# Input projections of a hybrid decoder layer: 576 tokens split as 256 and 320 columns in place of 288 and 288

## The reference, cut to what matters

```python
proj = jnp.einsum('btd,de->bte', x, w_in)            # d = 1024, e = 4096
q, k, v, g_att, gb, gc, hh, g_conv = jnp.split(proj, ...)   # 512 features each
o_att = _dilated_attention(q, k_all, v_all, offset).reshape(bsz, t, D_ATT)
att = o_att * jax.nn.silu(g_att)
u = gc * hh
y_conv = conv_w[0] * u_pad[:, 0:t] + ...              # width 3, causal, depthwise
z = gb * y_conv * jax.nn.silu(g_conv)
out = jnp.einsum('bte,ed->btd', jnp.concatenate([att, z], axis=-1), w_out)
y = _layer_norm(DEEPNORM_ALPHA * x + out, ln_g, ln_b)
```

## Time and profile before

| what | value |
|---|---|
| time, median of 3 runs (lowest to highest) | 361.42 us (359.41 to 361.47) |
| span of the profiled execution | 356.6 us |
| median time less that span | 4.8 us |
| TensorE busy | 347.5 us, 97% |
| VectorE busy | 201.2 us, 56% |
| ScalarE busy | 117.3 us, 33% |
| moved by DMA | 141.06 MB, 396 GB/s over the span |
| mean granted TensorE clock | 0.996 of full |

### The profile page before, as it was taken

One profiled execution on the slowest core, in us unless ns is written; L12 is line 12 of the kernel. 1 busy time (PEld: TensorE's weight loads), 2 busy tenths in 40 slices (PEclk: granted clock), 3 DMA queues, 4 the chain that ended last, 5 costly groups with the idle time before them and its releaser, 6 DMA issues.

```text
span 356.6 us, 7735 instructions
## 1 busy us (share of the span) xinstructions
PE 347.5 (97%) x3290; PEld 312.2 (88%) x3290; DVE 201.2 (56%) x379; ACT 117.3 (33%) x231; POOL 10.6 (3%) x28
## 2 busy tenths in 40 slices
PE   7999999999999999999999999999999999999992
PEld 5998988899998888999988889999788998888782
DVE  4534438854134649561346573821456499877775
ACT  5523324342144233421332423412533635230000
POOL 0000000000100000001000000000000000300000
PEclk9999999999999999999999999999999999999998
DMA  8999999999999999999999999999999999999992
GB/s 299 403 422 414 417 417 417 418 421 420 418 396 418 417 416 381 369 422 385 411 408 415 421 414 420 427 421 419 421 412 413 415 417 371 399 364 347 361 364 112
DMA packets 34549, 141.06 MB, mean 396 GB/s; under 512 B 3410, under 2 KB 3794, under 8 KB 32466
## 3 DMA queue, kind: packets, MB, share of 16 engines
q1 hardware_dynamic: 18050, 73.20, 51.0%
q10 hardware_dynamic: 16464, 67.37, 47.9%
HBM read 135.80 MB, written 71.86 MB: 582 GB/s over the span
## 4 chain that ended last, share of the span: by engine, by line
PE 96%; DVE 1%; DMA 1%; DVEq 0%; ACT 0%; issue 0%
PE pj_a L1137 11%; PE pj_b L1137 10%; PE pj_b L1139 10%; PE pj_a L1138 10%; PE pj_b L1138 10%; PE pj_a L1139 10%; PE sc L1261 5%; PE sc L1297 5%; PE px L1209 3%; PE po L1241 3%; PE px L1454 3%; PE px L1456 3%; PE px L1455 3%; PE pt L1227 2%; PE pt L1281 1%; DMA k_buf<-in_first 1%
## 5 line engine op out<-in xcount | busy, mean ns | idle before, releaser
L1137 PE MATMUL pj_a<-x_hi,w_hi 128*128 128x288 f32 x256 | 78.1, 305 | 1.2 <-DVE x_lo L779 1.2
L1137 PE MATMUL pj_b<-x_hi,w_hi 128*128 128x288 f32 x256 | 77.5, 303 | 0.0
L1138 PE MATMUL pj_a<-x_lo,w_hi 128*128 128x288 f32 x256 | 75.5, 295 | 0.0
L1138 PE MATMUL pj_b<-x_lo,w_hi 128*128 128x288 f32 x256 | 75.5, 295 | 0.0
L1139 PE MATMUL pj_b<-x_hi,w_lo 128*128 128x288 f32 x256 | 75.4, 294 | 0.0
L1139 PE MATMUL pj_a<-x_hi,w_lo 128*128 128x288 f32 x256 | 75.3, 294 | 0.0
L1137 PEld LDWEIGHTS pj_a<-x_hi,w_hi 128*128 128x128 f32 x256 | 48.0, 187 | 8.5 <-issue 6.2
L467 ACT CAST w_hi<-w_raw 128x1024 fp32r<-128x1024 f32 x30 | 31.4, 1046 | 65.5 <-PE pj_b L1139 32.8
L773 DVE TENSOR_TENSOR w_lo<-w_raw,w_hi 128x1024 fp32r<-128x1024 f32 x30 | 36.7, 1223 | 28.7 <-ACT w_hi L467 28.7
L1137 PEld LDWEIGHTS pj_b<-x_hi,w_hi 128*128 128x128 f32 x256 | 48.0, 187 | 2.3 <-issue 1.3
L1139 PEld LDWEIGHTS pj_b<-x_hi,w_lo 128*128 128x128 f32 x256 | 48.2, 188 | 0.0
(11 more groups left out here) (153 smaller groups left out, 434.9 us busy)
## 6 DMA issues: line engine op xcount, KB each, us to landing
k_buf<-in_k_used SPq DMA_DIRECT2D x16, 1280.0 KB, 13.8
v_buf<-in_v_used SPq DMA_DIRECT2D x40, 512.0 KB, 19.0
out_k_used_out<-in_k_used ACTq DMA_DIRECT2D x16, 1280.0 KB, 17.2
out_v_used_out<-in_v_used ACTq DMA_DIRECT2D x20, 1024.0 KB, 16.9
w_raw<-in_w_tiles SPq DMA_DIRECT2D x30, 512.0 KB, 13.0
out_k_rest_out<-in_k_rest ACTq DMA_DIRECT2D x12, 1024.0 KB, 11.6
out_v_rest_out<-in_v_rest ACTq DMA_DIRECT2D x12, 1024.0 KB, 12.7
wo_raw<-in_w_out SPq DMA_DIRECT2D x8, 512.0 KB, 20.9
```

The costliest lines, as they stand in the source:

```text
L1137: nc.tensor.matmul(out, w_hi[:, w], x_hi[:, c], start=(k == 0), stop=False)
L1138: nc.tensor.matmul(out, w_hi[:, w], x_lo[:, c], start=False, stop=False)
```

## The change

The two halves of tokens get the widths `WIDE` = (256, 320), with their edges at `EDGE` = (0, 256, 576). The loaded array `first` is laid out accordingly: the four first pieces hold 2 x 128 weight columns and 256 token columns for each of two blocks, the two last pieces 320 token columns for each of four blocks. `x_hi` and `x_lo` keep their size, and the second part starts at 8 x 256. All operations on a half take its width: the 24 matmuls of a tile and part, the copies out of `pj_a` and `pj_b`, the exponentials, the gates, the convolution's input and output. The prompt tokens in the second part, `HP_LEFT`, go from 224 to 256; the 64 sampled tokens stay in it. The number and the order of the instructions stay the same on every engine, and so do all waits and the bytes of each tensor.

```diff
-HALF = NT // 2
-HP_LEFT = SEQ - HALF
+WIDE = (256, 320)
+EDGE = (0, WIDE[0], NT)
+HP_LEFT = SEQ - EDGE[1]
...
-BLOCK = 2 * P + HALF
+BLOCK = 2 * P + WIDE[0]
...
         def x_cols(h, k0, k1):
 
-            return slice((h * KT + k0) * HALF, (h * KT + k1) * HALF)
+            return slice(KT * EDGE[h] + k0 * WIDE[h], KT * EDGE[h] + k1 * WIDE[h])
...
-                nc.scalar.copy(v_stage[:, 0:HALF], pj[0][:, 0:HALF]).then_inc(pj_read[0], 1)
+                nc.scalar.copy(v_stage[:, 0:EDGE[1]], pj[0][:, 0:WIDE[0]]).then_inc(pj_read[0], 1)
...
             def exp_gate(tile, h):
                 act.wait_ge(pj_done[h], tile + 1)
-                c = slice(h * HALF, (h + 1) * HALF)
-                nc.scalar.activation(rg[:, c], pj[h][:, 0:HALF], ACT.Exp, scale=-1.0).then_inc(g_exp, 1)
+                c = slice(EDGE[h], EDGE[h + 1])
+                nc.scalar.activation(rg[:, c], pj[h][:, 0:WIDE[h]], ACT.Exp, scale=-1.0).then_inc(g_exp, 1)
...
             def gate_half(i, gate, h):
 
-                c = slice(h * HALF, (h + 1) * HALF)
+                c = slice(EDGE[h], EDGE[h + 1])
...
-                    e = slice(h * HALF, min((h + 1) * HALF, SEQ))
+                    e = slice(EDGE[h], min(EDGE[h + 1], SEQ))
                     nc.vector.tensor_tensor(rg[:, e], rg[:, e], o_pr[:, e], ALU.mult).then_inc(g_step, 1)
...
             def product(slot, k, h, bank_):
-                out = pj[bank_][:, 0:HALF]
+                out = pj[bank_][:, 0:WIDE[h]]
```

More of the change, by code:

```diff
@@ L209, in x_loaded @@
                 return first_blocks(k0, k1)[:, :, 2 * P:]
[L210 removed]
+            return k_buf[:, KT * BLOCK + k0 * WIDE[1]:KT * BLOCK + k1 * WIDE[1]].rearrange("p (k t) -> p k t", t=WIDE[1])
         def x_part(x, h, k0, k1):
[L213 removed]
+            return x[:, x_cols(h, k0, k1)].rearrange("p (k t) -> p k t", t=WIDE[h])
         o_s = y_pad[:, 0:2 * P]
@@ L302, in _ @@
             for n, (h, k0, k1) in enumerate(X_CHUNKS):
-                c = slice(k0 * BLOCK, k1 * BLOCK) if h == 0 else slice(KT * BLOCK + k0 * HALF, KT * BLOCK + k1 * HALF)
+                c = (slice(k0 * BLOCK, k1 * BLOCK) if h == 0 else
+                     slice(KT * BLOCK + k0 * WIDE[1], KT * BLOCK + k1 * WIDE[1]))
                 sp.dma_start(k_buf[:, c], d["first"][:, c]).then_inc(x_in[n], 16)
@@ L536, in copy_q @@
                 act.wait_ge(pj_done[bank_], q_tile(i) + 1 if i else 1)
-                nc.scalar.copy(qk[:, 0:HALF], pj[bank_][:, 0:HALF]).then_inc(pj_read[bank_], 1)
+                nc.scalar.copy(qk[:, 0:EDGE[1]], pj[bank_][:, 0:WIDE[0]]).then_inc(pj_read[bank_], 1)
             def copy_kk(i):
@@ L542, in copy_kk @@
                     act.wait_ge(k_saved, 16 * i)
-                nc.scalar.copy(qk[:, NT:NT + HALF], pj[0][:, 0:HALF]).then_inc(pj_read[0], 1)
+                nc.scalar.copy(qk[:, NT:NT + EDGE[1]], pj[0][:, 0:WIDE[0]]).then_inc(pj_read[0], 1)
             split_x(4)
@@ L578, in copy_c @@
                 act.wait_ge(vt_done, i + 1)
-                nc.scalar.copy(gcs[:, h * HALF:(h + 1) * HALF], pj[h][:, 0:HALF]).then_inc(pj_read[h], 1)
+                nc.scalar.copy(gcs[:, EDGE[h]:EDGE[h + 1]], pj[h][:, 0:WIDE[h]]).then_inc(pj_read[h], 1)
             def exp_gate(tile, h):
                 act.wait_ge(pj_done[h], tile + 1)
-                c = slice(h * HALF, (h + 1) * HALF)
-                nc.scalar.activation(rg[:, c], pj[h][:, 0:HALF], ACT.Exp, scale=-1.0).then_inc(g_exp, 1)
+                c = slice(EDGE[h], EDGE[h + 1])
+                nc.scalar.activation(rg[:, c], pj[h][:, 0:WIDE[h]], ACT.Exp, scale=-1.0).then_inc(g_exp, 1)
             def exp_sample(i):
@@ L626, in split_mix @@
                 act.wait_ge(pj_read[0], W_TILES - (k0 == NHP))
-                if c1 > HALF:
+                if c1 > EDGE[1]:
                     act.wait_ge(pj_read[1], W_TILES)
@@ L891, in gate_half @@
                 row = (NHP if gate == 0 else 0) + i
-                nc.vector.tensor_tensor(mix[:, row * NT + h * HALF:row * NT + (h + 1) * HALF], pj[h][:, 0:HALF],
+                nc.vector.tensor_tensor(mix[:, row * NT + EDGE[h]:row * NT + EDGE[h + 1]], pj[h][:, 0:WIDE[h]],
                                         rg[:, c], ALU.mult).then_inc(pj_read[h], 1)
@@ L1528 @@
     w_first = w[:2 * P].reshape(2, P, KT, P).transpose(1, 2, 0, 3).reshape(P, KT, 2 * P)
-    xT = x.reshape(2, HALF, KT, P).transpose(3, 0, 2, 1)
-    a["first"] = np.concatenate([np.concatenate([w_first, xT[:, 0]], 2).reshape(P, -1), xT[:, 1].reshape(P, -1)], 1)
+    xT = x.reshape(NT, KT, P).transpose(2, 1, 0)
+    a["first"] = np.concatenate([np.concatenate([w_first, xT[:, :, 0:EDGE[1]]], 2).reshape(P, -1),
+                                 xT[:, :, EDGE[1]:].reshape(P, -1)], 1)
     a["w_tiles"], a["w_out"] = w[2 * P:], wo
```

20 lines of the change are left out of this document (10 added, 10 removed).

## The result

| kernel | median | lowest to highest | runs |
|---|---|---|---|
| before | 361.39 us | 358.72 to 363.9 | 20 |
| changed | 363.01 us | 360.12 to 366.76 | 20 |

A forecast was written before the change was run, and what follows sets the result against it. TensorE and the DMA were taken as full together. On the span of 356.6 us, -4.6 + 0.7 + 1.7 + 2.2 = 0.0 us, with 4.8 us around it: 361.4 us, range 355.5 to 363.7 us.

The forecast's parts named there:

- a gain of 4.6 us on TensorE: Projection rounds: 720 pairs of matmuls, each 6.4 ns cheaper, shorten TensorE by 4.6 us (bounds 14.4 and 0).
- two waits: Output projection: TensorE waits 1.7 us for w_out's low part and 2.2 us for the mixed tokens' low part.
- The distance at 256 columns: First part's projection matmuls: 113.4 ns each, taken from the output projection, 20.0 ns less than at 288 columns.
- rival C: Projections: distance linear in columns, nothing gained on TensorE; only the longer gate half counts, 0.3 us; 361.5 us, chance 0.10.
- The start: First two weight tiles: ScalarE's copy takes away the shorter first part's gain; the second part's 48 matmuls cost 0.7 us.
- The loads: Last w_out tile: the DMA has no idle time, so it lands when it did, cast at 301 to 302 us.
- VectorE's slack of 0.34 us: Before the second token tile: VectorE's low part is ready at 309.15 us, 0.34 us before TensorE begins at 309.49.
- The time around the span: Outside the profiled span of 356.6 us: 4.8 us, taken from the median of 361.42 us.
- A: Loads keep up with a TensorE that is 3.9 us ahead: 357.5 us, chance 0.16.
- B: Projection matmuls of 288 columns cost what 320 cost, TensorE 14.4 us ahead; 355 to 357 us if loads follow, chance 0.11.
- D: Waits of about 4 us let TensorE's clock fall, 2.3 us lost each: 363.7 or 366.0 us, chance 0.07.
- two signs named for a wrong forecast: Last w_out tile landing more than a microsecond earlier, or TensorE already waiting for w_in tiles in the rounds.

The follow-up runs named there:

- e1: Changed kernel with 224 single-pass matmuls added behind its end, at seven widths and four kinds of operands; one execution, 388.73 us with the added work.
- e4: Kernel before without its 60 copies of the caches from HBM to HBM (those outputs left unwritten); 358.60 us.
- e5: Changed kernel without the 60 copies of the caches (those outputs left unwritten); 359.28 us.
- e13: Changed kernel without cache copies, the last piece of x in two pieces and ScalarE's copy between their casts; 358.88 us.
- a0: Changed kernel measured again without any edit, for a second profile; 361.98 us, ratio 1.0017 to the kernel before.
- e17: Kernel before with GpSimd's two broadcasts of the layer norm's constants held back until VectorE is through with the chain; 360.54 us, ratio 0.9988.
- e11: Kernel before with the last piece of x in two pieces and ScalarE's copy between their casts; 361.45 us, ratio 1.0022.
- e14: Kernel before with five idle matmuls of 256 columns (0.60 us) ahead of the second part of x; 362.16 us, ratio 1.0008.
- e7: Kernel before with VectorE's last gate half moved ahead of the low parts of the last two w_out tiles; 360.92 us, ratio 1.002.
- e10: Changed kernel with the last piece of x in two pieces and ScalarE's copy between their casts; 361.25 us, ratio 1.0026 to the kernel before.
- e8: Changed kernel with VectorE's last gate half ahead of the low parts of the last two w_out tiles; 363.75 us, ratio 1.0089 to the kernel before.
- e16: Changed kernel with GpSimd's two broadcasts held back until VectorE is through with the chain; 361.16 us, ratio 0.9996 to the kernel before.
- b0: Kernel before measured again without any edit, for a second profile; 360.67 us, ratio 1.002.
- e3: Changed kernel's parts set to 224 and 352 columns; 364.41 us, ratio 1.0081 to the kernel before.
- a1: Changed kernel measured a third time without any edit; 362.21 us, ratio 1.0011 to the kernel before.
- after: First profiled execution of the changed kernel, without further edit; 363.11 us by the clock outside.
- e15: Changed kernel with the wide part first (320, 256) and without the cache copies (outputs unwritten); 358.95 us.

## Why the prediction was wrong

The forecast of no change missed by only 1.0 us, but its mechanism was wrong: a gain of 4.6 us on TensorE was to pay for the start and to be lost again in two waits. The gain did not exist, so that nothing paid for the start.

**The distance at 256 columns: the step that failed.** "These 256 columns have the same kind of operands, so I take 113.4 ns": they took 120.0 ns. With that, the gain of 6.4 ns a pair is 0.1 ns or nothing, and so are the 4.6 us. The row that the step rests on is no constant either. The same 48 matmuls of the output projection took 117.7 ns each in the second profiled execution of the kernel before:

```profile
346.51 0.28 PE L1454 MATMUL px<-wo,x_hi 128*128 128x256 f32 x1
...
352.04 0.28 PE L1456 MATMUL sc<-wo,x_lo 128*128 128x256 f32 x1
```

That is 5.53 us for 47 distances. Over the 20 profiles they stand at one of two values, 113.3 ns in 11 and 117.8 ns in 9, in executions of either kernel, and never at the 120.0 ns of the projections. Why there are two, and why neither is 120.0, no run settles: e1 exchanged the operands and found 118 to 121 ns, but in an execution of the slower value. The 4.6 us of the gain were worked out from one row of the quicker. The value for 320 columns, from the slope above 288, was right (147.0 against 146.7 ns). Of the steps on TensorE rival C had the true one, which the Trainium skill ("TensorE: Matmul & The Clock Gate", Back-to-back issue gap) implies by a rule linear in columns. Its constant does not fit: what stands above columns over 2.4 GHz in the projections is 13.3 ns, at 256, 288 and 320 alike, not 2.5. I had read the unequal 4.2 and 10.9 ns as evidence against a linear rule; they compared a row of the output projection with one of the projections, which do not lie on one line.

**The sum of rival C.** It had 0.3 us for the gate half against a slack of 0.34 us, and left out the 0.7 us of the start, which the main sum held. With it C gives 361.4 + 0.7 = 362.1 us, near the 0.68 us that e4 and e5 measure.

**The start.** "Gain nothing, and the 48 matmuls of the second part pay 0.7 us": right as a mechanism, somewhat large in size. The wait for ScalarE's copy came as described (0.61 us), the second part began 0.2 to 0.3 us earlier than before, and the net was 0.4 us; e13 confirms that the copy makes most of it. In a0 the first part itself was slow, and there was no wait for the copy.

**The loads.** "It lands when it did": not seen. The eighth cast came at 305.27, 304.56 and 304.91 us in the changed kernel, at 301.44 and 302.43 us in the kernel before. But e17, e11 and e14, with halves of 288, had it at 303.68, 304.28 and 304.65 us (e7: 301.17), and e10, with 256 and 320, at 302.90 us (e8 and e16: 303.74 and 303.88). Single profiles scatter by 3 us there, so a later landing by the change is not shown. The longer waits of ScalarE for w_in tiles (35.2 us against 19.5) are no sign of it either: e17, with halves of 288, has 30.2 us. The waits that I forecast in front of the output projection came, though not from a TensorE that was ahead: 1.23 us at 294.87 and 1.66 us at 314.19 us.

**VectorE's slack of 0.34 us.** It was read from a chain which GpSimd's broadcast had already lengthened, by 1.1 us in the quick execution (the addition at 303.67 us took 1.40 us, and 0.30 us in e17) and by 2.0 us in the usual one. The prediction's two longer steps (0.3 us for 320 columns) were right in size; the collision was not in it.

**The time around the span.** 4.8 us in the forecast, 1.8 us in the changed kernel and the same in b0 (360.76 less 359.0). The forecast of 361.4 us stood on the median, so its error here cancelled: that was luck, and it hid that a usual execution already waits.

**The rest.** A (the loads keep up) and B (288 costs as 320) are refuted by the distances. D did not happen in any of the changed kernel's three profiles: the granted clock is 1.00 from 305 to 318 us, where its waits lie. But its mechanism is real, and nearer than I had it: in e8 a wait of 1.88 us, not 4 us, stood ahead of a stretch at half clock, which cost 1.7 us where D had 2.3. Neither of the two signs named for a wrong forecast came (an earlier last load, waits for w_in tiles in the rounds); the distances of 120 and 147 ns named for C did. The range of 355.5 to 363.7 us held the time.

**A version that beats both.** No version is shown to. The wide part first came to 0.9972 and 0.9987, weighted 0.998 (0.996 to 1.000), and one line that moves the broadcasts to 0.9988. None lies clearly further from 1 than the unchanged kernel's own 1.002.

## What to carry to other kernels

Splitting a matmul stream unevenly gains nothing where the distance is linear in columns, and loses as soon as one part falls below the width where it goes flat (here between 224 and 256 columns). Before a duration is carried from one stage to another, look at it in a second execution, and measure it in the stage that will use it: 113.4 ns was one of two values in its own stage, and not the value of the other. Where a variant is slower than its waits explain, look at the granted clock behind the longest wait. Where VectorE's step on the last chain is longer than the same shape elsewhere, look at GpSimd in that stretch before blaming the load.

## What the runs showed of the hardware

- In the projections a stream of 128 by 128 single-pass fp32r matmuls ran at columns/2.4 GHz + 13.3 ns at 256, 288 and 320 columns (120.0, 133.4, 146.7 ns); at 384 columns 173 ns (e1), at 512 columns 228.9 ns, and at 111 to 112 ns for 128, 192 and 224 columns (e1, e3; two of e1's groups at 105 and 115 ns).
- The 48 matmuls of 256 columns in the output projection took 113.3 ns each in 11 profiled executions and 117.8 ns in 9.
- After a wait of 1.88 us TensorE's granted clock stood at 0.50 from 309 to 312.3 us although it was busy again (e8): 1.7 us lost. Behind waits of 1.11 to 1.78 us in the same place it stayed at 1.00.
- With the first matmuls at 213 ns in place of 120 (a0), TensorE was 0.7 us later at the second part of x.
- A VectorE subtraction of two SBUF operands took 1.52 to 2.14 us beside GpSimd's broadcasts (a0, a1, after, b0, e10) and 1.23 us without them, and a 0.3 us addition of a constant 1.40 to 1.42 us; the broadcast took up to 2.24 us in these places and 1.30 us in e16, away from them. The Trainium skill ("SBUF — State Buffer", Who interferes with whom) says that a VectorE instruction with two SBUF inputs, or one in a two-port mode, and a GpSimd instruction that reads SBUF exclude each other for a whole instruction. e16 and e17 agree as far as that the two engines lengthen each other: with the broadcasts moved, all lengths are plain. That one waits for a whole instruction of the other, they do not test.
- Without the copies of the caches, the executions of one kernel agreed within 0.9 us (358.18 to 359.05; 0.5, 1.6 and 1.9 us in e5, e13 and e15) where with them they spread over 5 us (358.72 to 363.9): most of the scatter of this kernel comes with the copies.
